# A decoder layer's expert stage on one core: the three weight chunks kept in SBUF from the stage's head serve the thirtieth job's turn instead of the twentieth's

## What is computed

```
logits = hf @ w_router + b_router
top_v, top_e = top_k(logits, 4);  top_w = softmax(top_v)
# the rows of each expert, in blocks, go through that expert:
gu   = xb @ w_gate_up[e] + b_gate_up[e]          # 1024 -> 2048
gate = minimum(gu[:, 0::2], 7.0);  up = clip(gu[:, 1::2], -7.0, 7.0)
act  = (up + 1.0) * gate * sigmoid(1.702 * gate)
ys   = act @ w_down[e] + b_down[e]               # 1024 -> 1024
out  = zeros.at[row_tok].add(ys * row_w)
x    = x + gate2 * out
```

## Time and profile before

| | |
|---|---|
| median of 3 runs | 1679.5 us (1678.61 to 1679.74) |
| span of the profiled execution | 1674.4 us |
| PE busy in it | 1620.8 us, 97% |
| DVE, ACT, POOL busy | 577.2, 423.4, 280.7 us |
| weight loads, up and down, of 1 MB | 253 and 128, median 19.2 and 20.4 us to landing |
| loads into `sb_kept`, of 1 MB | 3, median 6.9 us to landing |
| row additions and gathers in the loop | 32 and 31, median 10.7 and 8.7 us to landing |

### The profile page before, as it was taken

How to read it: one execution, slowest core, us unless ns; L and a number is a source line. 1 busy time by engine, 2 the same in 40 slices (tenths; PEclk the granted TensorE clock), 3 DMA queues, 4 the chain that set the end, 5 groups by cost and what they waited for, 6 DMA issues and landing times.

```text
span 1674.4 us, 44999 instructions
## 1 busy us (share of the span) xinstructions
PE 1620.8 (97%) x19112; PEld 900.9 (54%) x19112; DVE 577.2 (34%) x1341; ACT 423.4 (25%) x869; POOL 280.7 (17%) x355
## 2 busy tenths in 40 slices
PE   8999896999999989999999999999999999999996
PEld 6668896677888843344334433443443344334433
DVE  2448464755345553122212211321222132113212
ACT  4343433675223402121112111111211121111111
POOL 4000620101000020221211122111212211221211
PEclk9999999999999989999999999999999999999998
DMA  9940000312345479999999999999999999999983
GB/s 392 363 185 1 3 5 11 122 55 101 114 138 201 164 302 377 403 401 398 398 393 403 397 397 394 400 396 387 404 355 394 389 404 399 393 401 401 399 341 122
DMA packets 87479, 489.80 MB, mean 293 GB/s; under 512 B 15093, under 2 KB 17202, under 8 KB 34504
## 3 DMA queue, kind: packets, MB, share of 16 engines
q1 hardware_dynamic: 79708, 471.54, 70.8%
q0 software_dynamic: 7504, 16.80, 4.3%
q10 hardware_dynamic: 188, 0.30, 0.0%
HBM read 478.61 MB, written 19.55 MB: 298 GB/s over the span
## 4 chain that ended last, share of the span: by engine, by line
PE 63%; DVE 0%; issue 0%; POOLq 0%; DVEq 0%
PE bank L2324 39%; PE bank L2335 19%; PE bank L2315 2%; PE bank L2348 1%; PE bank L2336 1%; PE bank L2325 1%; DVE sb_y L2561 0%; PE bank L2358 0%; DVE sb_biased L2542 0%; POOLq L2201 0%; PE bank L2368 0%; PE bank L2363 0%; DVE sb_aT L2538 0%; DVE sb_aT L2539 0%; DVEq L2606 0%
## 5 line engine op out<-in xcount | busy, mean ns | idle before, releaser
L2324 PE MATMUL bank<-sb_w_raw,sb_xT 128*32 128x512 f32 x4554 | 665.4, 594 | 0.4 <-DVE sb_biased L2542 0.4
L2325 PE MATMUL bank<-sb_w_raw,sb_xT 128*32 128x512 f32 x1518 | 664.5, 594 | 0.0
L2324 PEld LDWEIGHTS bank<-sb_w_raw,sb_xT 128*32 128x32 f32 x4554 | 184.3, 110 | 431.2 <-issue 425.7
L2335 PE MATMUL bank<-sb_w_raw,sb_aT 128*32 128x256 f32 x4608 | 337.9, 379 | 2.0 <-DVE sb_aT L2539 2.0
L2336 PE MATMUL bank<-sb_w_raw,sb_aT 128*32 128x256 f32 x1536 | 337.5, 380 | 0.0
L2335 PEld LDWEIGHTS bank<-sb_w_raw,sb_aT 128*32 128x32 f32 x4608 | 187.7, 110 | 130.9 <-DVE sb_y L2561 2.3
L2542 DVE TENSOR_TENSOR sb_biased<-bank,sb_bias 128x512 f32<-128x512 f32 x96 | 60.3, 684 | 476.3 <-PE bank L2325 364.4
L2336 PEld LDWEIGHTS bank<-sb_w_raw,sb_aT 128*32 128x32 f32 x1536 | 166.3, 110 | 0.0
L2325 PEld LDWEIGHTS bank<-sb_w_raw,sb_xT 128*32 128x32 f32 x1518 | 164.5, 110 | 0.0
L2440 ACT COPY sb_bias<-sb_last_quarter 32x1536 f32<-32x1536 f32 x32 | 47.0, 1468 | 403.9 <-POOL sb_last_quarter L2497 403.9
L2492 POOL TENSOR_TENSOR sb_tick<-sb_ones 128x1 f32<-128x1 f32 x93 | 34.0, 366 | 557.4 <-issue 424.6
(11 more groups left out here) (512 smaller groups left out, 2245.1 us busy)
## 6 DMA issues: line engine op xcount, KB each, us to landing
sb_w_raw<-in_w_gate_up_dram SPq DMA_DIRECT2D x253, 1024.0 KB, 19.2
sb_w_raw<-in_w_down_dram SPq DMA_DIRECT2D x128, 1024.0 KB, 20.4
sb_ring<-in_w_in_dram SPq DMA_DIRECT2D x7, 2048.0 KB, 13.5
sb_x<-in_ada_w_dram SPq DMA_DIRECT2D x8, 1024.0 KB, 9.3
sb_mod<-in_ada_w_dram SPq DMA_DIRECT2D x8, 1024.0 KB, 8.0
sb_ring<-in_ada_w_dram SPq DMA_DIRECT2D x6, 1024.0 KB, 14.4
sb_x<-in_x_dram SPq DMA_DIRECT2D x2, 2048.0 KB, 9.6
sb_ring<-in_w_out_dram SPq DMA_DIRECT2D x2, 2048.0 KB, 7.5
```

Source lines behind the costliest of these rows:

```text
L2324: te.matmul(up_bank[r][at, :], g.xT[:, k, at], raw[:, s, 512 * r:512 * r + 512], start=first, stop=last)
L2325: mm = te.matmul(up_bank[r][CAP:P, :], g.xT[:, k, STRIP * r:STRIP * r + STRIP], raw[:, s, 512 * G:2048], start=first, stop=last)
L2335: te.matmul(down_bank[j][at, 0:256], g.aT[:, k, at], g.w_raw[:, s, 1024 * r + 256 * j:1024 * r + 256 * j + 256], start=first, stop=last)
```

## The change

One constant: the turn in which the three kept chunks serve. With it the expert changes whose chunks are loaded at the head (30 instead of 20), the turn in which SP leaves out three loads (29 instead of 19), and the length of the two loops before and behind the written-out turn. No instruction's form and no tile changes.

```
-        KEPT_TURN, KEPT = 19, 3
+        KEPT_TURN, KEPT = 29, 3
```

## The result

The changed kernel takes 1684.03 us (median of 20 runs), the kernel before 1679.62 us in as many runs beside it. The ratio of the runs is 1.0028, 95% interval 1.0021 to 1.0036: 4.7 us more, 3.5 to 6.0 (the two medians alone differ by 4.4). That is slower by more than 0.2%, and in the range; the forecast was 1683.5 us.

A forecast was written before the change was run, and what follows sets the result against it. The prediction took PE to bound every turn of the expert loop, with SP's load queue just behind. Its terms, 0 + 0 + 0 + 4.0 us, added to 1679.5 us gave 1683.5 us, range 1679.2 to 1686.0.

The forecast's parts named there:

- The bound and the mechanism: Expert loop: PE bounds every turn at 32.85 us; SP's load queue is slower, melting the loads' lead 0.7 to 0.8 us a turn.
- Terms 1 to 3: Expert 30's loads at the stage's head, moved loop ends, three fewer loads from turn 29 on: 0 us each.
- Term 4: Turns 19 to 28: three more loads in SP's queue delay later loads 7.4 us; PE waits 4.0 us, between 3.0 and 4.3.
- the shift by three loads: Turn 28: POOL transfers stay in time, so load n lands when load n+3 lands now; shortfall 4.3 us.
- The way to the median: Whole program: the runs' median is 5.1 us above the profiled span, and this is carried over to the forecast.
- A: Loads' lead is larger where nothing is recorded, so not slower, 1679.5 us; chance 0.25 with its partial forms.
- B: Loads' lead is smaller where nothing is recorded, up to the full 7.4 us visible, 1685 to 1687 us; chance 0.15.
- C: PE's granted clock drops in the last waiting turn, adding up to 5 us, about 1688 us; chance 0.03.
- What was to be seen: Profile after: weight-load waits together about 4 us between 1330 and 1590 us, flights 28 to 30 us from turn 22 on.
- the rule that I set against the row: Expert loop: a 358 GB/s HBM load limit would need 35.1 us a turn, costing some 20 us over ten turns.

The follow-up runs named there:

- the fewer rows: Changed kernel with each job's row addition taking 32 of its 96 rows, the rest left out of the output; ratio 0.9983 to the kernel before.
- the slower PE: Changed kernel with the eight row transposes of each turn done three times over; 1717.0 us in one run.
- later issues: Changed kernel where SP, ahead of each load, also waits for the use of the place two further on; ratio 1.0035 to the kernel before.

## Why the prediction was right, point by point

**The bound and the mechanism.** Right. PE was the bound, the queue came second by 0.7 us a turn, and the lead was the account between them. Turn 9 against turn 29 shows that time on the account is what counts, one chunk against three that the sum on it counts, the fewer rows and the slower PE that it is the difference of two rates.

**Terms 1 to 3.** 0 each, right. Loading expert 30 at the head, moving the loops' ends and the three loads fewer at the end left turns 0 to 21 and 29 to 30 at 32.85 us. With the kept chunks in turn 9 the loops' ends lie elsewhere again and nothing is lost.

**Term 4.** The form was right, the size too small: 4.0 us forecast, 5.5, 6.4 and 3.5 us in three profiles, 5.1 on average. The times gave 4.7 us (3.5 to 6.0) in the first comparison, 5.5 (3.4 to 7.9) and 6.9 (4.5 to 9.4) in the two others; that the first came so close to 4.0 is in part luck. The step that was off is the pace of the queue in the waiting turns, which I put at 0.6 us a turn over PE's, from one execution, with a total between 3.0 and 4.3. In the profiles of the changed kernel turns 22 to 28 were 33.64, 33.77 and 33.36 us long on average; the turns that waited (from turn 23, 22 and 24 on, without the 0.1 us in turn 22 of the first) were 0.87, 0.92 and 0.70 us over PE's. The upper end of my bounds, the shift by three loads, was the better of the two, and still below two of the three. The first wait came in turns 22, 22 and 24, not in turn 21, and the lead in turn 18 decides much of it: 5.3 us of lead there (at the two chunks named above) went with 6.4 of waits, 5.9 with 5.5, 7.4 with 3.5.

Whether waiting turns need more of the queue than free ones can be read from each execution's own free turns. In the first profile the flights of up loads issued for turn 10 and for turn 20, ahead of any wait, were:

```profile
L1879 SPq DMA_DIRECT2D sb_w_raw<-in_w_gate_up_dram x8: 333/333/337, 929.9 to 948.8; - x8
DMA to landing us min/median/max: 16.5/16.8/17.6
...
L1879 SPq DMA_DIRECT2D sb_w_raw<-in_w_gate_up_dram x8: 332/333/1117, 1258.4 to 1277.4; - x8
DMA to landing us min/median/max: 24.7/24.9/26.0
```

That is 0.8 us a turn. Taken over the same loads of each turn (the second to fifth up chunk, where recorded), the three profiles have 0.82, 0.83 and 0.76 between these turns, beside the 0.87, 0.92 and 0.70 of their waiting turns. The kernels without kept chunks, with one and with later issues have 0.85, 0.66 and 0.83 in the free turns just ahead of their waits and 0.83, 0.63 and 0.81 in the waiting ones. All six agree within 0.1, to either side, so no run shows that waiting by itself needs more of the queue. My pace came from behind the relief of turn 19: in turns 20 to 28 the kernel before rose by 0.63 a turn (0.54 in its second profile), in turns 10 to 18 by 0.84 (0.83). The changed kernel has no relief in turn 19 and went on at about the pace of the turns ahead of it. Why the pace was lower behind that relief stays open; behind the one in turn 9 it was hardly so (0.76 in turns 10 to 18).

**The way to the median.** I carried 5.1 us from span to median as something that lies around the span. Only 1.8 us do (the first profiled run of the changed kernel took 1683.26 us at a span of 1681.5). The other 3.3 us mean that the profiled execution was a fast one; the start of turn 0 spreads widely enough for that, but that it was this isn't shown. The forecast adds its 4.0 us to the median of before, so the 5.1 fall out of the difference and did no harm.

**The rivals.** A (a larger lead outside the profile) is out: the time rose in all three comparisons of the changed kernel. B (a smaller one) is out for the kernel before, whose two profiles have no waits. C (the clock) didn't come where I looked, in the waiting turns. It came at the end, where I had taken one row as proof that 2.0 us of waiting leave the clock alone: behind the same wait the clock fell in two of twelve profiles.

**What was to be seen.** Flights of 24, then 28 to 30 from turn 22 on, then some 21 us: 24.4, then 27.0 in turn 22 and 28 only from turn 24 on, 20.9. Waits together about 4 us by the list: 3.9, which stand for 5.5 of delay. Turn 30's transposes at 1642.6: 1644.06.

The run also answers the rule that I set against the row, a limit of about 358 GB/s for loads from HBM (the Trainium skill, DMA: Bandwidth & Descriptors, section Bandwidth): over the seven waiting turns the engines moved 385 GB/s, of which the loads' queue alone had 368, and ten turns without relief cost 5 us, not 20.

No version here is faster than the kernel before with its whole work done: its turns are PE's own 32.85 us, without a wait for a load that more lead could take away.

## What to carry to other kernels

Where a load queue is slightly slower than the engine it feeds, a transfer left out of it is a payment into the loads' lead: it is worth about the same at any time before the lead runs dry, as long as loads are still queued up behind each other, and it brings back nothing of the waits that have happened, so pay early. Read the flight of the loads turn by turn, not the engine's waits, to see such a margin melt while the engine still shows none. Take the rate at which it melts from more than one execution.

## What the runs showed of the hardware that I had not expected

In the expert loop nearly every DMA issue of SP took 0.33 us with up to eight loads of 1 MB on their way. With nine or ten (an estimate, from the landings that are recorded) more than half of the changed kernel's issues were longer, 2.0 us in the median of the long ones and up to 5.0 us, as if the queue had no more room; in the kernel before, with nine on their way at most, none was. In the runs here SP had nothing else to do, and the run without long issues was no faster.

The clock after a wait of PE differs from execution to execution: the 2.05 us ahead of the last down chunks were followed by 3.4 us at 0.50 in two of twelve profiles, 1.7 us each, and by none in the others; waits of 0.1 to 1.1 us among full turns were followed by none in any.
